# A ninth 2 MB expert slot, and the first stage's 12 columns of beta and decay multiplied with v's second rows

## What is computed

```python
q_a, k_a, v_a, z_a, b_a, a_a, q_b, k_b, v_b = jnp.split(x @ w_in, EVEN_SPLITS, axis=-1)
beta = jax.nn.sigmoid(b_a)
g = -jnp.exp(a_log) * jax.nn.softplus(a_a + dt_bias)
```

```python
for e in range(N_EXPERTS):
    hidden = jax.nn.silu(t @ w_gate[e]) * (t @ w_up[e])
    out = out + combine[:, e:e + 1] * (hidden @ w_down[e])
```

## Time and profile before

| | |
|---|---|
| median of 3 runs | 1760.88 us |
| lowest and highest run | 1760.47, 1765.22 us |
| profiled execution, first to last instruction (its span) | 1759.8 us |
| mean granted TensorE clock in it | 0.980 of full speed |
| PE, PEld busy | 1648.0 us (94%), 1226.0 us (70%) |
| DVE, ACT, POOL busy | 937.4 us (53%), 627.9 us (36%), 228.9 us (13%) |
| moved by DMA | 429.45 MB, 244 GB/s over the span |

### The profile page before, as it was taken

One profiled execution on the slowest core, in us unless ns is written; L12 is line 12 of the kernel. 1 busy time (PEld: TensorE's weight loads), 2 busy tenths in 40 slices (PEclk: granted clock), 3 DMA queues, 4 the chain that ended last, 5 costly groups with the idle time before them and its releaser, 6 DMA issues. The chain is left out here.

```text
span 1759.8 us, 25741 instructions
## 1 busy us (share of the span) xinstructions
PE 1648.0 (94%) x10372; PEld 1226.0 (70%) x10372; DVE 937.4 (53%) x1668; ACT 627.9 (36%) x1050; POOL 228.9 (13%) x217
## 2 busy tenths in 40 slices
PE   9999998999999989999999989997789999899966
PEld 8788875699988544899888864442379898643422
DVE  1285664688642565788554766131166967732212
ACT  1035322466531224566446541110144456411101
POOL 0000000054202121263101302000000300020000
PEclk9999999999999999999999999998999999999989
DMA  8322186445553666455424766999954655699996
GB/s 328 144 96 96 66 337 268 170 166 216 192 215 122 238 275 251 162 197 193 168 96 144 301 249 260 421 421 421 390 217 144 201 225 177 259 408 421 421 420 265
DMA packets 50336, 429.45 MB, mean 244 GB/s; under 512 B 5788, under 2 KB 6048, under 8 KB 9248
## 3 DMA queue, kind: packets, MB, share of 16 engines
q1 hardware_dynamic: 47232, 417.59, 61.0%
q0 software_dynamic: 2256, 7.88, 1.3%
q10 hardware_dynamic: 720, 2.23, 0.3%
HBM read 426.62 MB, written 1.05 MB: 243 GB/s over the span
## 5 line engine op out<-in xcount | busy, mean ns | idle before, releaser
L88 ACT ACTIVATE arena<-ps 128x384 f32<-128x384 f32 (+5 forms) x221 | 96.4, 436 | 512.3 <-PE ps L82 305.5
L82 PE MATMUL ps<-ringx,arena 128*64 128x512 f32 (+1 forms) x1088 | 251.0, 623 | 29.6 <-DMA ring<-in_mu 19.7
L82 PE MATMUL ps<-xsplit_f,wsplit_f 128*128 128x256 f32 x2112 | 256.0, 284 | 4.2 <-ACT xsplit_f L88 2.6
L82 PEld LDWEIGHTS ps<-xsplit_f,wsplit_f 128*128 128x128 f32 x2112 | 254.1, 192 | 6.6 <-ACT xsplit_f L88 4.2
L82 PE MATMUL ps<-ring,arena 128*64 128x512 f32 (+2 forms) x768 | 238.7, 618 | 15.7 <-DMA ringx<-in_md 6.9
L91 DVE TENSOR_TENSOR wsplit_f<-ring,wsplit_f 128x1024 fp32r<-128x1024 f32 x132 | 180.2, 1369 | 70.3 <-ACT wsplit_f L88 70.3
L82 PEld LDWEIGHTS ps<-ringx,arena 128*64 128x64 f32 (+1 forms) x1088 | 75.3, 130 | 168.7 <-issue 157.7
L82 PE MATMUL ps<-xTs,ring 128*128 128x256 f32 (+1 forms) x960 | 186.0, 353 | 2.2 <-ACT xTs L88 2.2
L82 PEld LDWEIGHTS ps<-xTs,ring 128*128 128x128 f32 x960 | 161.4, 191 | 23.3 <-issue 4.8
L88 ACT ACTIVATE wsplit_f<-ring 128x1024 fp32r<-128x1024 f32 x132 | 138.1, 1051 | 57.4 <-PE ps L82 56.5
L91 DVE TENSOR_TENSOR ringlo<-ring,ringhi 128x1024 fp32r<-128x1024 f32 x88 | 120.4, 1384 | 58.6 <-ACT ringhi L88 58.3
(11 more groups left out here) (204 smaller groups left out, 2315.8 us busy)
## 6 DMA issues: line engine op xcount, KB each, us to landing
ring<-in_wu SPq DMA_DIRECT2D x22, 2048.0 KB, 8.5
ringx<-in_mg SPq DMA_DIRECT2D x44, 1024.0 KB, 15.5
ringx<-in_mu SPq DMA_DIRECT2D x44, 1024.0 KB, 17.9
ring<-in_ada SPq DMA_DIRECT2D x20, 2048.0 KB, 8.7
ringx<-in_md SPq DMA_DIRECT2D x32, 1024.0 KB, 17.3
ring<-in_md SPq DMA_DIRECT2D x32, 1024.0 KB, 23.7
ring<-in_wd SPq DMA_DIRECT2D x10, 2048.0 KB, 8.2
ring<-in_mg SPq DMA_DIRECT2D x20, 1024.0 KB, 15.6
```

The source lines that it names most:

```text
L82: return self.e.matmul(o, l, r, start=start, stop=stop, skip_group_check=True)
L88: return self.e.activation(o, i, f, **k)
```

## The change

- `WIDE` is 9: the experts get a ninth slot (number 8, the sixth of `ringx`). `EXTRA` and `ABOVE` name it behind the slots that could be filled early before: fourth in line for stage 5, third for stage 7.
- Room for it: the descriptors' share of each partition goes from 16384 to 1024 bytes; `posi`, the positions that retention's rotation needs, is no longer a buffer but lies in `gate`; `wba` (96 columns) is gone from the parameters.
- The 12 gate columns are appended to `wev2`, which has 268 columns now, and `wev2` is loaded and multiplied ahead of `wev`. ACT copies the 12 columns of each half from bank "vb1" to `small`. Bank "ba", its 16 matmuls and DVE's copy are gone. DVE copies "vb0" after it has made the decay.

```diff
-WIDE = 8
+WIDE = 9
...
-    out = [("we", 6), ("we", 7), ("we", 8), ("wev",), ("wev2",)] + [("we", j) for j in range(6)]
+    out = [("we", 6), ("we", 7), ("we", 8), ("wev2",), ("wev",)] + [("we", j) for j in range(6)]
...
-EXTRA = [(5, 6, 7, 3, 4), (6, 7, 4, 5, 3)]
-ABOVE = [(5, 6, 7), (6, 7)]
+EXTRA = [(5, 6, 7, 8, 3, 4), (6, 7, 8, 4, 5, 3)]
+ABOVE = [(5, 6, 7, 8), (6, 7, 8)]
...
-    posi = sb("posi", 256, I32)
+    posi = gate[:, 0:256].bitcast(I32)
...
+            proj_rows(("wev2",), "vb1", 268)
             proj_rows(("wev",), "vb0", 512)
-            proj_rows(("wev2",), "vb1", 256)
-            b = bank("ba")
-            wba = C("wba").rearrange("p (k n) -> p k n", k=8)
-            for h in range(2):
-                for k in range(8):
-                    r = mm(b[:, 12 * h:12 * h + 12], xT[:, k, h * 128:h * 128 + 128], wba[:, k, :], k == 0, k == 7)
-            r.then_inc(s_pe, t.did("ba"))
...
-            for h in range(2):
-                evac_rows("vb0", h, E.vbt[:, h, 0:512])
-            v.note("vbt")
-            v.wait_ge(*t("ba"))
-            copy(small[:, 0:24], ps("ba")[:, 0:24]).then_inc(s_dve, v.did("free", "ba"))
-            v.note("ba")
             ba = two(small[:, 0:24])
             v.wait_ge(*a("beta_exp"))
...
                 .then_inc(s_dve, v.did("decay"))
+            for h in range(2):
+                evac_rows("vb0", h, E.vbt[:, h, 0:512])
+            v.note("vbt")
             v.wait_ge(*t("gam"))
...
             for h in range(2):
+                a.wait_ge(*t("vb1", h))
+                copy(small[:, 12 * h:12 * h + 12], ps("vb1", h)[:, 256:268]).then_inc(s_act, a.did("ba"))
                 evac_rows("vb1", h, E.vbt[:, h, 512:768])
...
-    nc = _bacc.Bacc("TRN2", target_bir_lowering=False, num_devices=1)
+    nc = _bacc.Bacc("TRN2", target_bir_lowering=False, num_devices=1, dynamic_dma_scratch_size=1024)
```

More of the change, by code:

```diff
@@ L367 @@
           ("lnw", 1), ("lbg", 2), ("rgn", 16), ("adab", 96), ("lng", 64), ("lnb", 64), ("c", 8), ("dl", 4), ("rb", 4),
-          ("lwg", 256), ("rw", 128), ("wba", 96), ("wgd", 128)]
+          ("lwg", 256), ("rw", 128), ("wgd", 128)]
 ROWS = [("alog", 6), ("dtb", 6), ("rtb", 16)]
@@ L490, in width @@
     def width(name):
-        return 2048 if name[0] in ("wev2", "wdl") else 4096
+        return {"wev2": 2144, "wdl": 2048}.get(name[0], 4096)
     xtl = xlo[:, :, :].rearrange("p a (k n) -> p (a k) n", n=256)
@@ L2471, in ret @@
             ang, kq = Q.rtmp[0][:, 0:256], Q.rtmp[1][:, 0:256]
-            ki = posi[:, :]
+            ki = posi
             c1, c2 = 6.28125, 2 * math.pi - 6.28125
@@ L2687, in even @@
             ba = small[:, 0:24].rearrange("p (t n) -> p t n", t=2)
-            a.wait_ge(*v("ba"))
             act(small[:, 24:36].rearrange("p (t n) -> p t n", t=2), ba[:, :, 0:6], ACT.Exp, scale=-1.0) \
@@ L3063, in ret @@
             stage_begins(5)
-            a.dma_start(posi[:, :], ins["pos"].broadcast_to([128, 256])).then_inc(s_dec, 16)
+            a.dma_start(posi, ins["pos"].broadcast_to([128, 256])).then_inc(s_dec, 16)
             a.dma_start(Q.dec, ins["dec"]).then_inc(s_dec, 16)
@@ L3502 @@
     ins["wev"] = tiles(we[:, 4620:5132], 8, 512)
-    ins["wev2"] = tiles(we[:, 5132:5388], 8, 256)
+    ins["wev2"] = tiles(_np.concatenate([we[:, 5132:5388], we[:, 3072:3084]], 1), 8, 268)
     ins["woe"] = rowtiles(a["w_out_even"][0], 4)
@@ L3544 @@
         "lwg": pad(a["gla_w_gate"][0]), "rw": tiles(a["router_w_2"], 8, 16)[0],
-        "wba": tiles(we[:, 3072:3084], 8, 12)[0], "wgd": tiles(wo[:, 3072:3088], 8, 16)[0],
+        "wgd": tiles(wo[:, 3072:3088], 8, 16)[0],
     }
```

## The result

| | kernel before | changed kernel |
|---|---|---|
| median of the runs | 1762.35 us (1760.47 to 1765.22, 4 runs) | 1747.16 us (1745.53 to 1750.48, 4 runs) |
| ratio, with its 95% interval | | 0.9918 [0.9902, 0.9934] |
| span of the profiled execution | 1759.8 us | 1744.7 us |
| mean granted clock of TensorE in it | 0.980 | 0.984 |

The change is worth 14.5 us (11.6 to 17.3 by the interval). The forecast was 6.4, and its range ended at 1750.8: the direction was right, the size was not.

The account below looks back on a forecast made before the run. Full DMA was taken to bound the two expert stages, PE and what feeds it the rest. Gains of 3.76, 1.36 and 1.25 us, 6.37 off 1760.88, gave 1754.5 us, range 1750.8 to 1759.0.

Parts of the forecast that it names:

- The ninth slot: Expert stages 5 and 7: one half matrix lands early, 2.49 us less a DMA gap, gaining 1.36 and 1.25 us.
- The first stage: Even mixer's start: 12-column block gone 3.49, wait before "gam" gone 0.59, wider matmuls cost 0.32; gain 3.76 us.
- Other edits: `posi` in `gate`, last matrices in `ringx`: no cost or gain; POOL's smaller descriptor share left to rival 6.
- Rival 3: Expert stages: a quicker stream ends before SP's reads do, gains only 0.64 and 0.53; total 4.9, 1756.0 us; chance 0.08.
- the gap behind the reads: Expert stages: SP's 12 expert-number reads outlast seven halves, leaving DMA without work for 1.13 and 1.24 us.
- the rule set against the sum: Trainium skill's 2.0 us plus bytes over 436 GB/s: stage gains 0.69 and 0.57, sum 5.0, giving 1755.9 us.
- the dip: Sign in stages 5 and 7: DMA falls between last `md` and first `mg`, worth 1 to 1.5 us at 421 GB/s.
- Rival 1: Expert stages: SP's reads overlap or flow resumes at once, 2.49 us per stage; total 8.7, 1752.2 us; chance 0.15.
- Rival 2: Expert stages: a whole matrix counts in each, 9.96 us together; total 13.7, 1747.2 us; chance 0.05.
- Rival 4: First stage: DVE keeps part of the gain, 1.4 to 3.76 us lost; 1755.9 to 1758.3 us; chance 0.12.
- Rival 5: Slot is filled no earlier than before and stage one gains nothing; 1760.9 us; chance 0.03.
- Rival 6: POOL's DMAs block on 1024 bytes of descriptors, 5.1 us per pair; slower by 8.9, 1769.8 us; chance 0.05.

Follow-up runs that it names:

- e6_sbuf_back: e3_eight_slots with unused buffers of 96 and 256 columns, putting every buffer where it lay in e1_scratch; 1754.27 us, ratio 0.9957 to the kernel before.
- e1_scratch: The kernel before with only the DMA scratch cut to 1024 bytes, so every buffer lies 15360 bytes lower; 1763.05 us against 1762.56, ratio 1.0001.
- e9_slots_moved: e1_scratch with 160 unused columns (640 bytes) ahead of the five extra expert slots alone; 1756.83 us against 1762.29 for the kernel before, ratio 0.997.
- e12_all_moved: e1_scratch with 160 unused columns behind `cp`, moving everything behind it; 1756.38 us, ratio 0.9963 to the kernel before.
- e2_first_stage: The kernel before with the first-stage edits alone, including `posi` in `gate`; eight slots and the scratch as before; 1750.01 us, ratio 0.9922.
- e3_eight_slots: The changed kernel without the ninth slot, first stage and scratch as in the change; 1751.53 us, ratio 0.9926 to the kernel before.
- e7_lazy_ids: The changed kernel with SP reading each expert's id just before the first transfer needing it; 1743.74 us against 1761.31 for the kernel before, ratio 0.9897.
- e16_pad512b: e1_scratch with 128 unused columns (512 bytes) ahead of the extra expert slots; single run, 1759.14 us against 1760.15 for the kernel before.
- e8_both_halves: e7_lazy_ids with both halves of place 8's `mu` sent before the halves of place 12; 1742.23 us, ratio 0.9891 to the kernel before.
- e10_arena_moved: e1_scratch with 160 unused columns ahead of the whole expert arena, the five slots behind it included; 1757.84 us, ratio 0.9969 to the kernel before.

## Why the prediction was wrong, step by step

The step that failed is the pricing of the smaller edits at nothing: they moved the expert slots in SBUF, and the rate of the stream, taken as fixed at 421 GB/s, rose to 426. That is 4.0 to 4.7 us of the 8.1 missed. The ninth slot was priced right; the first stage was 0.8 short, and a loss of clock in the old one, 1.7 on average, was not seen.

- **The first stage (3.76 us).** Right in mechanism, short by 0.77. The block alone is exact: "TP" moved by 3.17, which is 3.49 less 0.32. Behind it "gam" moved by 4.02 and the transposes by 4.12, and the wait for `arena` fell from 0.96 to 0.54, which makes the 4.53 that all seven traces with the edit show (4.52 to 4.54). DVE was named as what could be late next; it moved with PE, as forecast, and the transposes begin without a wait.
- **A TensorE clock that I could not see.** The repeated runs of e6_sbuf_back, which has the new first stage and the old rate, give 7.6 us (5.1 to 10.0), more than 4.5. The old first stage has a loss that the profiled execution shown before happened not to have. These are windows of e1_scratch, whose first stage is the old one:

```profile
76.00:84.00 8.00, 8.00 (x31) 5.41 (x30) 4.28 (x15) 1.48 (x7) 0.00 (x0) 0.59 0.45 195
84.00:92.00 8.00, 8.00 (x30) 6.75 (x30) 6.81 (x13) 2.92 (x7) 0.00 (x0) 0.77 0.00 1
```

  and the same of the kernel before and of the changed one:

```profile
76.00:84.00 8.00, 7.41 (x43) 5.59 (x44) 4.42 (x15) 1.48 (x7) 0.00 (x0) 1.00 0.49 211
```

```profile
76.00:84.00 8.00, 8.00 (x46) 7.01 (x46) 6.79 (x14) 1.29 (x5) 0.00 (x0) 1.00 0.52 220
```

  The clock is at its lower level, 1.2 GHz, for part of those windows of e1_scratch; it falls at 77.5, right behind the 12-column block (in all six such traces between 75.8 and 77.9). Of 13 traces with the old first stage six show 0.50 to 0.62 there, six 1.00, and one 0.95; of the seven with the new one all show 1.00. It costs 3.0 to 4.7 us (the stretch 46 to 106; 3.1 in the rows e1, e9 and e12), with six in 13 about 1.7 on average. That the block of narrow matmuls is what brings it on is likely by its place, but not shown. Even that it goes with the first-stage edits is not certain from the traces alone: if the edits had nothing to do with it, all six would still fall among the 13 of the 20 traces about once in 23 times. The 7.6 us of e6_sbuf_back speak for it as well.
- **"Other edits", priced at nothing.** This is the step that failed. "`posi` in `gate`: same DMA, same wait, no cost" and, in the part on the first stage, "`cp` 48 KB smaller, and PE had waited for neither: nothing" are true of the instructions, but the two take 1408 bytes out from under the expert slots, which so start at a multiple of 256 bytes. The stream's rate, 421 GB/s, was taken over as a constant of the kernel. About 190 full microseconds a stage at 421 need 188 at 426 (190 x 5 / 426 = 2.2 us), and e9_slots_moved and e12_all_moved gain 2.1 to 2.5 in each stage, e2_first_stage and e3_eight_slots 1.7 to 2.4: **4.0 to 4.7 us in the two stages that had no term**. The repeated runs put it at 5.3 (e9_slots_moved) and 5.5 us (e3_eight_slots less e6_sbuf_back, 0.9957 - 0.9926), with wide intervals.
- **Rival 3** had a quicker stream in it, but only for its effect on the gap behind the reads, where it costs. That it also shortens the whole stream was left out, there and in the rule set against the sum, which had a quicker rate still; no full slice of any run is above 428 GB/s.
- **The ninth slot (1.36 and 1.25).** Right, and the sum of the two is 2.6 in both: 1.6 and 1.0, with SP's halves, the missing eighth half behind the release and the dip as forecast. Rival 1 is refuted by the dip, and e7_lazy_ids puts its price at the 1.13 and 1.24 worked out. Rival 2, whose 1747.2 is nearly the measured time, is refuted as a mechanism: e3_eight_slots has all but 1.4 us of the gain without the slot. That its number was met is luck. The forecast of when the `mu` halves go out, 3.8 us earlier, missed as the time did: it was 6.0 in stage 5, and 11.8 in stage 7 against 5.1.
- **Rivals 4, 5 and 6** did not happen: transposes at 88.24, POOL's issues at 1.15 us, and scratches of 1024 and 2048 bytes alike in time.

The account: 4.5 (first stage) + 1.7 (clock, on average) + 4.1 (rate, as e2_first_stage and e3_eight_slots have it beside the same first stage) + 2.6 (slot) = 12.9 us, inside 11.6 to 17.3. What is left of the measured 14.5 is smaller than the interval and stays open. The profiled executions differ by 15.1, and of these the clock in 76:84 is no part, as both had 1.00 there. 11.2 are first stage, rate and slot; 1.8 lie in 1268 to 1340, where the kernel before had a late rise of the clock at the start of retention:

```profile
1288.00:1296.00 8.00, 4.90 (x24) 4.88 (x24) 3.51 (x7) 4.19 (x9) 1.70 (x3) 0.64 0.66 246
```

e1_scratch and e16_pad512b gain 2.6 us there with no edit that reaches it. The rest, 2.1 us, lies in stretches whose work the edits leave as it was but for the place of `posi` (106 to 1058, 1340 to 1540), and I can't place it.

**A version that beats both.** e8_both_halves stands at 1742.23 us and e7_lazy_ids at 1743.74; their intervals overlap, so which of the two is better is open. e7_lazy_ids is a few lines from the change and 0.9897 [0.9878, 0.9915] of the kernel before. Its interval overlaps a little with that of the change too (0.9918 [0.9902, 0.9934]); that it is better rests also on its six runs, the slowest of them (1745.33 us) below the fastest of the change (1745.53), and on the 1.2 and 1.3 us in the two stages.

## What to carry to other kernels

When an edit adds or drops a buffer, list the start of every buffer behind it, modulo 256 bytes, before pricing it at nothing: here 640 bytes of padding ahead of the DMA's landing slots gave 5.3 us of 1762 (2.8 to 7.9), and the expert stream is the place to look because it is the only one where DMA is full. The measured rate of 421 GB/s belonged to this layout, and another layout had 426, so a term for "the same bytes, at another rate" belongs in every sum with a DMA-bound stage. One trace is one draw: take terms of 3 us that a single profile shows, or fails to show, from several executions, and compare the granted clock of the stretch before comparing its time.

## What was unexpected of the hardware

- Packets of 8 KB to SBUF took 309 ns with the slots on a multiple of 256 bytes and 314 on average off it, at full DMA share, in all 20 traces; one aligned buffer among two was nearly enough (310.9 with only the ring aligned, 309.7 with only the extra slots). Outside the full stretches, with the same addresses, most packets were at 309 ns in every trace. DMA's share reads 1.01 at either rate, so the share does not tell the loss; the GB/s does.
- Twelve of the 13 programs with the old first stage, which run the same instructions up to there, show TensorE's clock in 76:84 either at 0.50 to 0.62 or at 1.00, six each, and the loss stays in the stages behind it. One profile can't tell which of the two the median holds. The thirteenth, e10_arena_moved, was granted 0.95 in 60:92, apart from both.
